# A decoder layer whose mixing stage is planned on TensorE: attention steps ranked ahead of delta-rule steps, with a new order of tiles

## What is computed

```python
n = rms_norm(h, ln_mix_pre)
da_q, da_k, da_v, dn_q, dn_k, dn_v, dn_z, dn_b, dn_a, ca_q, gate_logits = split(n @ w_in)
y_a = diff_attention(da_q, da_k, da_v, rel_bias, ...)         # 8 heads, two softmax maps each
cq, ck, cv = split(short_conv(concat(dn_q, dn_k, dn_v)))      # causal, width 4, silu
y_b = rms_norm(gated_delta_rule(cq, ck, cv, g, beta), dn_norm_g) * silu(dn_z)   # 8 heads
y_c = memory_attention(ca_q, mk, mv)                          # 4 heads, 256 memory tokens
mixed = sum(sigmoid(gate_logits) * einsum('bsiw,iwd->bsid', [y_a, y_b, y_c], w_branch))
h = h + rms_norm(mixed @ w_out, ln_mix_post)
h = h + rms_norm(square(relu(rms_norm(h, ln_ff_pre) @ w_ff1)) @ w_ff2, ln_ff_post)
```

## Time and profile before

| what | value |
|---|---|
| median of 3 runs | 1394.61 us (1393.35 to 1395.2) |
| the profiled execution | 1393.79 us, of which 1392.0 us span |
| PE busy | 1366.7 us, 98% of the span |
| DVE busy | 774.4 us, 56% |
| ACT busy | 483.3 us, 35% |
| POOL busy | 199.7 us, 14% |
| mean granted TensorE clock | 0.991 of full speed |
| DMA | 143.14 MB moved, 103 GB/s |
| chain that ended last | PE 91%, DVE 7%, ACT 1% |

### The profile page before, as it was taken

How to read it: one execution, slowest core, us unless ns; L and a number is a source line. 1 busy time by engine, 2 the same in 40 slices (tenths; PEclk the granted TensorE clock), 3 DMA queues, 4 the chain that set the end, 5 groups by cost and what they waited for, 6 DMA issues and landing times.

```text
span 1392.0 us, 24486 instructions
## 1 busy us (share of the span) xinstructions
PE 1366.7 (98%) x10516; PEld 1132.3 (81%) x10516; DVE 774.4 (56%) x1277; ACT 483.3 (35%) x778; POOL 199.7 (14%) x140
## 2 busy tenths in 40 slices
PE   8899999999999999999999999999899999999998
PEld 8689887887888888888788878888888888888886
DVE  6796227844765957679544634553455522355333
ACT  5354433433534435435344222112433212222231
POOL 1112000020000200002001322232322200022010
PEclk9999999999999999999999999999989999999998
DMA  5154322222222221232222466645213232223331
GB/s 212 61 174 140 107 69 91 84 70 70 68 71 89 92 70 60 64 106 69 86 77 92 152 211 184 194 137 183 75 47 106 91 100 97 92 91 92 90 91 60
DMA packets 46434, 143.14 MB, mean 103 GB/s; under 512 B 4944, under 2 KB 7416, under 8 KB 46328
## 3 DMA queue, kind: packets, MB, share of 16 engines
q1 hardware_dynamic: 46328, 141.59, 31.8%
HBM read 126.88 MB, written 16.27 MB: 103 GB/s over the span
## 4 chain that ended last, share of the span: by engine, by line
PE 91%; DVE 7%; ACT 1%; issue 1%; DMA 1%; SPq 0%; DVEq 0%; ACTq 0%
PE acc L1713 25%; PE acc L1715 24%; PE acc L1714 24%; PE ps_d L1867 2%; PE ps_a L1788 2%; PE ps_a L1799 1%; DVE w_lo L1296 1%; PE ps_d L1829 1%; DVE conv_y L1398 1%; PE ps_a L1778 1%; PE ps_a L1767 1%; PE ps_d L1839 1%; PE ps_d L1843 1%; PE ps_d L1845 1%; PE ps_a L1794 1%
## 5 line engine op out<-in xcount | busy, mean ns | idle before, releaser
L1713 PE MATMUL acc<-n_hi,w_hi 128*128 128x512 f32 (+1 forms) x984 | 395.6, 402 | 3.8 <-DVE n_lo L1586 2.4
L1715 PE MATMUL acc<-n_hi,w_lo 128*128 128x512 f32 (+1 forms) x984 | 382.2, 388 | 0.0
L1714 PE MATMUL acc<-n_lo,w_hi 128*128 128x512 f32 (+1 forms) x984 | 381.9, 388 | 0.0
L1296 DVE TENSOR_TENSOR w_lo<-w_raw,w_hi 128x1024 fp32r<-128x1024 f32 x200 | 284.6, 1430 | 147.8 <-ACT w_hi L998 147.0
L998 ACT CAST w_hi<-w_raw 128x1024 fp32r<-128x1024 f32 x200 | 209.6, 1049 | 437.8 <-PE acc L1715 437.6
L1713 PEld LDWEIGHTS acc<-n_hi,w_hi 128*128 128x128 f32 x984 | 186.7, 190 | 44.5 <-issue 5.1
L1715 PEld LDWEIGHTS acc<-n_hi,w_lo 128*128 128x128 f32 x984 | 186.5, 189 | 40.5
L1714 PEld LDWEIGHTS acc<-n_lo,w_hi 128*128 128x128 f32 x984 | 187.1, 190 | 35.1 <-issue 0.5
L1715 PE MATMUL acc<-h_hi,w_lo 128*128 128x512 f32 x256 | 101.0, 395 | 0.0
L1713 PE MATMUL acc<-h_hi,w_hi 128*128 128x512 f32 x256 | 101.0, 395 | 0.0
L1714 PE MATMUL acc<-h_lo,w_hi 128*128 128x512 f32 x256 | 101.0, 395 | 0.0
(11 more groups left out here) (336 smaller groups left out, 1933.1 us busy)
## 6 DMA issues: line engine op xcount, KB each, us to landing
w_raw<-weights SPq DMA_DIRECT2D x200, 512.0 KB, 3.6
gate_scratch<-gate_st SPq DMA_DIRECT2D x24, 256.0 KB, 2.9
g_in<-gate_scratch SPq DMA_DIRECT2D x24, 256.0 KB, 4.0
y_raw<-y_scratch SPq DMA_DIRECT2D x16, 256.0 KB, 3.7
x_tok<-x SPq DMA_DIRECT2D x4, 512.0 KB, 5.5
y_scratch<-y_st SPq DMA_DIRECT2D x4, 512.0 KB, 3.1
y_scratch<-d_ET SPq DMA_DIRECT2D x4, 512.0 KB, 3.8
y_scratch<-y_st SPq DMA_DIRECT2D x8, 256.0 KB, 2.4
```

The lines of the kernel that those rows point to most:

```text
L1296: V_.tensor_tensor(w_lo[:, t % SPL], w_raw[:, t % RAW], w_hi[:, t % SPL].bitcast(F32), ALU.subtract).then_inc(lo_ready, 1)
L1713: mm(bank, wh, hi_of(k), start=start and k == 0, stop=False)
L1714: mm(bank, wh, lo_of(k), start=False, stop=False)
L1715: last = mm(bank, wl, hi_of(k), start=False, stop=stop and k == KT - 1)
```

## The change

Two things: in `rank`, TensorE's family of attention steps stands ahead of the delta-rule steps, and `ORDER` is another list. It has the same kinds of tiles, as many of each. The new list moves the first gate tile to the second place and a second one behind the first pair of z tiles, z tiles of pair 1 and 2 forward, and the z tiles of pair 3 further back.

```diff
-ORDER = [("conv", 0), ("z", 0), ("gate", 1), ("mem", 0), ("cq", 0), ("gate", 1), ("cq", 1), ("conv", 1),
...
-         ("head", 2), ("gate", 1), ("head", 3), ("head", 4), ("conv", 3), ("gate", 1), ("z", 2), ("head", 5),
-         ("gate", 4), ("head", 6), ("head", 7), ("z", 3), ("gate", 14)]
+ORDER = [("conv", 0), ("gate", 1), ("z", 0), ("gate", 1), ("mem", 0), ("gate", 1), ("cq", 0), ("cq", 1),
...
+         ("head", 2), ("gate", 1), ("head", 3), ("head", 4), ("conv", 3), ("z", 2), ("head", 5), ("head", 6),
+         ("gate", 1), ("head", 7), ("gate", 6), ("z", 3), ("gate", 12)]
...
-    rank = {"PE": ("delta", "attn", "main"), "ACT": ("hi", "evac", "delta", "attn", "fin", "finz"),
+    rank = {"PE": ("attn", "delta", "main"), "ACT": ("hi", "evac", "delta", "attn", "fin", "finz"),
```

More of the change, by code:

```diff
@@ L85 @@
 ISSUE_US = {"T1": 2.4, "Za": 2.4, "Wb": 4.6, "Z5": 1.2, "W5": 1.7}
-ORDER = [("conv", 0), ("z", 0), ("gate", 1), ("mem", 0), ("cq", 0), ("gate", 1), ("cq", 1), ("conv", 1),
-         ("cq", 2), ("gate", 1), ("cq", 3), ("head", 0), ("conv", 2), ("head", 1), ("gate", 1), ("z", 1),
-         ("head", 2), ("gate", 1), ("head", 3), ("head", 4), ("conv", 3), ("gate", 1), ("z", 2), ("head", 5),
-         ("gate", 4), ("head", 6), ("head", 7), ("z", 3), ("gate", 14)]
+ORDER = [("conv", 0), ("gate", 1), ("z", 0), ("gate", 1), ("mem", 0), ("gate", 1), ("cq", 0), ("cq", 1),
+         ("conv", 1), ("z", 1), ("cq", 2), ("cq", 3), ("head", 0), ("conv", 2), ("head", 1), ("gate", 1),
+         ("head", 2), ("gate", 1), ("head", 3), ("head", 4), ("conv", 3), ("z", 2), ("head", 5), ("head", 6),
+         ("gate", 1), ("head", 7), ("gate", 6), ("z", 3), ("gate", 12)]
 def attn_steps():
```

## The result

The changed kernel takes 1398.51 us (median of 19 runs, 1394.38 to 1401.78), the kernel before 1391.23 us on the same chip (19 runs, 1390.35 to 1395.24). The ratio of the runs is 1.0040, with a 95% interval of 1.0033 to 1.0048: slower by 5.6 us (4.6 to 6.7; the two medians lie 7.3 us apart, but I go by the ratio of the runs, which has an interval). I had forecast 1394.3 us, no change, and a range of 1392.0 to 1397.0. That is wrong: the median lies outside the range, and the loss is twice what can be told from no change. The three runs of the kernel before that I had (median 1394.61) also lay high in its spread, and so does the profiled execution of before, 2.6 us above the median of its 19 runs.

The account below looks back on a forecast made before the run. TensorE's own work plus about 4 us of waits was taken to bound the mixing stage. 1393.79 + 0.15 (borders) - 0.5 (T1 wait) = 1393.4 us profiled, 1394.3 us against the median; range 1392.0 to 1397.0.

Parts of the forecast that it names:

- the work of the moved steps: TensorE, mixing stage: a step costs its own rows wherever it stands, so moving it costs 0.
- the wait at T1 of pair 3: TensorE's wait for DVE there falls from 0.82 to about 0.3 us with fewer gate scalings: -0.5, bounds 0 and -0.82.
- the queues: SP queue: moved tiles take loads, scalings and stores along; 14 quarter tiles after pair 3's last step still cover: 0.
- What bounds the kernel: Mixing stage: time is TensorE's own work, which an order cannot change, plus about 4 us of waits, which it can.
- the borders: First weight matmul after a 32x32 solve step costs +0.20 us; 32 such borders before, 35 now: +0.15, bounds -0.2 and +0.6.
- The wait before the q transposes: Pair 0: same 14 us of TensorE and same DVE list ahead, so the wait stays: 0, bounds -1.4 and +0.6.
- The scores ahead of dA: Pair 1: cross-attention head 3 scores pass before dA; some 2 us are left over before Za, cost 0.
- past the mixing stage nothing moves: Stages after the mixing stage: the change leaves everything there in place.
- The slower one: Rival: six gate scalings in pair 3's solve each delay a DVE pass TensorE needs; 3.7 us, 1398.0 us, chance 0.10.
- The rule does nothing: Rival: only tile places count, attention and delta steps seldom being ready together; both waits stay, 1394.8 us, chance 0.13.
- The sum: Whole kernel: 1393.79 + 0.15 - 0.5 = 1393.4 us for the profiled execution, 1394.3 us against the median.

Follow-up runs that it names:

- second profile: Unchanged copy of the changed kernel, profiled again: ratio 1.0040 to the kernel before, span 1397.6 us.
- The shifts: Dummy matmuls added in TensorE's first wait: changed kernel by 64 instructions 1.0027, by 128 1.0031; kernel before by 64 1.0026; changed kernel with both repairs 1.0019 and 1.0018.
- half kernels: Kernel before with only the new rank: 1408.3 us, ratio 1.0107; changed kernel with the old rank, so new tile order alone: 1404.5 us, ratio 1.0088.

## Why the prediction was wrong

Three terms failed, in the prediction's own words the work of the moved steps (put at 0, measured +2.4 us of stops), the wait at T1 of pair 3 (put at -0.5, measured +0.94) and the queues (put at 0, measured +0.95).

*What bounds the kernel.* Right as far as it went: TensorE's own work and a few waits. The step that failed is the sentence that the time is a sum of work, "which an order cannot change", and waits. There was a third part that the profile before did not show as time: the arrival of TensorE's instructions, and, in some executions, a fourth: 6.8 us at the lower clock.

*Work of the moved steps, 0, and the borders, +0.15.* The first term was the largest miss: the new order costs 2.4 us (second profile 3.3) in stops for packets, since the same 32x32 bursts fall on other borders of the 256-instruction packets. I had asked only what a border costs the neighbouring matmul. The shifts show that the kernel before was at zero by luck: with 64 instructions more, the one shift of it that I tried, it loses 3.6 us.

*The wait at T1 of pair 3, -0.5.* Wrong in sign: +0.94. The parts I counted were nearly right: of the operations that I had looked at DVE saved some 0.5 us, and TensorE came as much later as I had said. I left out that DVE's maximum, starting 2.1 us later behind the v transposes, moved the small operation L1445 from the tail of GpSimd's own pass L903 to its start: 1.85 us for 0.35. I had counted the gate scalings and not the delta passes of GpSimd, though the earlier trace rows hold the w_lo pass that took 2.92 us beside one of these. The profile before even held the same collision in full, one operation of the q norm at the start of the pass L906, between rows that I had read:

```profile
639.53 1.90 POOL L906 TENSOR_TENSOR d_K<-d_K,e_tail 128x1024 f32<-128x1024 f32 x1
...
639.56 1.90 DVE L1286 SCALAR_TENSOR_TENSOR smd<-smd 128x8 f32<-128x8 f32 x1
```

Releasing L903 sooner took 0.9 us off the wait.

*The wait before the q transposes, 0.* Right: 1.2 before, 1.1 after. Its cause, L903 over the convolution, was not what I named.

*The scores ahead of dA.* Right: no wait there.

*Queues and DMAs, 0; "past the mixing stage nothing moves".* Wrong by 0.95 us in the first profile and more in the second: I counted 14 quarter tiles behind the last step of pair 3 as cover for its DVE pass and store, and forgot what follows them on the same queue, the reloads of y, which now stand between gate stores.

*The rivals.* The slower one had its price nearly right (3.7 us) by luck, and its mechanism wrong: the solve of pair 3 with its gate tiles has no new wait for DVE. "The rule does nothing" fell with the two half kernels: with the old tile order it costs 15 us, with the new one it saves some 7 (1.0088 against 1.0040).

*The sum.* 2.4 + 0.94 + 0.95 = 4.3 us in the first profile explains its 3.9. For the 5.6 us of the runs, the larger terms of the second profile (its transposes of L1911 come 8.3 us later than in the first profile before) and the fall of the clock at 743 us in four of nine profiles are enough; how much of each belongs to a typical run is not settled. Behind the mixing stage no effect of the order shows: from L1911 to the end I measured 390.3, 390.4, 389.7 and 388.3 us with the order of before, 390.2 and 387.6 us in the two profiles of after. That part differs by over 2 us between two executions of the same kernel, of which the time at half clock around 1010 to 1027 us is a piece (10.2 us in the first profile of after, 6.8 in the second).

## What to carry to other kernels

Where a busy engine runs bursts of very small instructions, look at its "instruction" queue: lay the packets' ends beside the bursts, before believing that a reorder is free, and shift the program by some dummy instructions to learn how much of a difference is the place in the packets. Before moving work on one engine, list what GpSimd does in those microseconds, all of it, since the smallest DVE operation can take as long as the pass beside it. And this schedule and its priority rule were tuned together: each half of the change alone told nothing of the whole.

## What was not expected of the hardware

- TensorE's instructions come during the run, in packets of 256. In 16 profiles the instruction with remainder 193 never started sooner than 1.2 us after the end of the packet that I pair it with, and all stops without a releaser in the mixing stage, 0.2 to 3.2 us long, had it start 1.2 to 1.6 us after. That this instruction stands for the first of the packet, and the 63 missing places for a queue in between or for instructions without a record, is my reading. Most packets take 0.88 to 1.9 us; when one is asked for can't be seen, nor why it starts late.
- Stops of 2.5 and 3.2 us in such a burst were followed by half the clock for 6.8 and 3.4 us; one of 2.3 us (at 353.26) and one of 2.0 us (at 698.40 with the rank alone) were not. At 743 us (four of nine profiles) and at 752 and 712 us (the half kernels) it fell with no stop or wait just ahead.
- A DVE operation of 0.17 us took 1.85 us beside a GpSimd pass of 1.90 us, a maximum read from PSUM was not held up by one (the three pieces took 1.62 us with and without it).
